# Heads of 64 dimensions alternate over both row halves and two banks, and the decay's steps stand one place later in block 2

## The reference

```python
# block 1, in each of 2 layers: the indexer of the sparse attention
qi = partial_rope(iq.reshape(bsz, seq, 4, 64), positions)         # IDX_HEADS 4, IDX_DIM 64
ki = partial_rope(rms_norm(ik, g_kidx[l]), positions)             # one key of 64 for all heads
rel = relu(einsum('bthd,bsd->bths', qi, ki) * 64 ** -0.5)
score = einsum('bths,bth->bts', rel, w_idx) * 4 ** -0.5           # then top 64 of the keys
# block 2, in each of 2 layers: the decay of the gated delta rule
g = -exp(A_log) * softplus(a + dt_bias)                           # (256 tokens, 4 heads)
gc = cumsum(g in chunks of 64 tokens)
decay = exp(where(incl, gc[t] - gc[j], -inf));  k_end uses exp(gc[-1] - gc)
# and, beside it, silu(causal_conv(q, k, v)) with 4 taps; MoBA attention, 4 heads of 64
```

## Time and profile before

| | |
|---|---|
| median of 3 runs | 1377.88 us (1376.53 to 1378.09) |
| the profiled execution | 1379.59 us, of which the span is 1377.80 us |
| PE busy | 1350.5 us, 98% of the span |
| DVE busy | 1039.6 us, 75% |
| ACT busy | 754.8 us, 55% |
| mean granted clock of PE | 0.996 of full speed |

### The profile page before, as it was taken

The page is one execution under the profiler, slowest core; times in us unless marked ns, Lnnn a source line. Parts: engine busy times, 40 slices in busy tenths (PEclk is TensorE's granted clock), DMA queues, the critical chain, the costliest instruction groups (busy, mean ns, idle before and its releaser), DMA issues. The chain is left out here.

```text
span 1377.8 us, 26466 instructions
## 1 busy us (share of the span) xinstructions
PE 1350.5 (98%) x10812; PEld 1270.2 (92%) x10812; DVE 1039.6 (75%) x1777; ACT 754.8 (55%) x1163; POOL 46.2 (3%) x48
## 2 busy tenths in 40 slices
PE   8999999999999999999999999999999999999998
PEld 8899999998999989899999989999989899888996
DVE  6999898677766667999897767666777746768565
ACT  6544656556445455544567546444558546576463
POOL 0000000000000000000000000000000110001100
PEclk9999999999999999999999999999999999999999
DMA  8555444564655465655355554555463324243231
GB/s 283 184 202 171 135 153 158 180 214 157 203 191 184 144 223 169 210 171 186 100 184 159 196 196 154 185 193 195 162 196 109 120 63 141 94 172 108 78 100 70
DMA packets 108992, 223.77 MB, mean 162 GB/s; under 512 B 6180, under 2 KB 17700, under 8 KB 108872
## 3 DMA queue, kind: packets, MB, share of 16 engines
q1 hardware_dynamic: 106736, 219.12, 48.0%
q10 hardware_dynamic: 2136, 2.96, 0.7%
HBM read 221.01 MB, written 1.06 MB: 161 GB/s over the span
## 5 line engine op out<-in xcount | busy, mean ns | idle before, releaser
L1749 DVE TENSOR_TENSOR wlo<-ring,whi 128x1024 fp32r<-128x1024 f32 (+3 forms) x430 | 498.4, 1181 | 191.6 <-ACT whi L1166 161.9
L1166 ACT ACTIVATE whi<-ring 128x1024 fp32r<-128x1024 f32 (+3 forms) x430 | 433.0, 1026 | 367.1 <-PE bank L497 230.8
L497 PE MATMUL bank<-hhi,whi 128*128 128x256 f32 x2016 | 279.6, 280 | 6.6 <-ACT sgb L1426 4.8
L506 PE MATMUL bank<-hhi,wlo 128*128 128x256 f32 x2016 | 280.3, 281 | 0.0
L497 PE MATMUL bank<-hlo,whi 128*128 128x256 f32 x2016 | 276.9, 279 | 0.0
L497 PEld LDWEIGHTS bank<-hhi,whi 128*128 128x128 f32 x2016 | 253.6, 189 | 10.1 <-ACT sgb L1426 5.5
L506 PEld LDWEIGHTS bank<-hhi,wlo 128*128 128x128 f32 x2016 | 252.6, 188 | 3.7 <-issue 3.2
L497 PEld LDWEIGHTS bank<-hlo,whi 128*128 128x128 f32 x2016 | 253.2, 189 | 0.0
L467 PE MATMUL bank<-w 64*64 64x64 f32 (+5 forms) x1376 | 104.4, 249 | 1.2 <-DMA w<-in_flip 0.8
L1929 DVE SCALAR_TENSOR_TENSOR w<-w,par 128x256 f32<-128x256 f32 x240 | 98.1, 480 | 0.0
L519 PE MATMUL bank<-whi,hhi 128*128 128x512 f32 (+2 forms) x256 | 96.5, 378 | 0.0
(11 more groups left out here) (309 smaller groups left out, 1538.1 us busy)
## 6 DMA issues: line engine op xcount, KB each, us to landing
ring<-in_w_in SPq DMA_DIRECT2D x100, 1024.0 KB, 5.1
ring<-in_w_ffn_down SPq DMA_DIRECT2D x22, 1024.0 KB, 5.1
ring<-in_w_ffn_gate SPq DMA_DIRECT2D x20, 1024.0 KB, 5.1
ring<-in_w_ffn_up SPq DMA_DIRECT2D x20, 1024.0 KB, 5.1
ring<-in_w_merge SPq DMA_DIRECT2D x8, 1024.0 KB, 5.2
ring<-in_w_out SPq DMA_DIRECT2D x8, 1024.0 KB, 4.9
ring<-in_w_oc SPq DMA_DIRECT2D x4, 1024.0 KB, 5.4
ring<-in_w_od SPq DMA_DIRECT2D x4, 1024.0 KB, 5.2
```

What stands on the lines that cost most here:

```text
L497: done = e.matmul(o, wh[:, k, cols(u)], s_[:, k0 + k, :], stop=False, skip_group_check=True, start=opens and k == 0 and s_ is sh and u % 2 ...
L506: done = e.matmul(o, wl[:, k, cols(u)], sh[:, k0 + k, :], start=False, stop=closes, skip_group_check=True)
L1166: e.activation(part_of(whi, j), part_raw(j), ACT.Copy).then_inc(*up("hi.a"))
L1749: e.tensor_tensor(part_of(wlo, j), part_raw(j), part_of(whi, j), ALU.subtract).then_inc(*up("lo.v"))
```

## The change

First, in the indexer of block 1, two query heads are turned at once as one block of 128 columns, and the key is copied twice side by side (a new DVE copy for each of the two token blocks, into `kk`) and turned as a third block. So `iT` holds heads 0 and 2 in its slots 0 and 1 in the lower 64 partitions, heads 1 and 3 in the upper 64, and the key in both. Each token block needs one bank and one evacuation by ACT where it had two. Second, the index scores alternate between the two halves of the partitions and between two banks. Third, `logits_p` takes both banks ahead and, for MoBA, alternates in the same way. Fourth, in block 2 the third and fourth step of the decay stand at places 12 and 13 where they stood at 11 and 12.

```diff
--- before.py
+++ after.py
@@ -93,7 +93,7 @@
         "bias": [5, 5, 5, 6],
         "taps": [12, 20, 34],
         "others": [28, 34, 41, 41, 53],
-        "decay": [10, 10, 11, 12],
+        "decay": [10, 10, 12, 13],
         "delta": [17, 18, 20, 20, 30, 30, 36, 37, 39, 41, 43, 46, 46, 48, 48, 50, 51, 52, 53, 54, 55, 62, 65, 66, 66],
         "latent": [26, 29, 30, 34, 36, 37, 39, 43, 46, 53, 54, 65, 66],
         "outs": [58, 66, 71, 71],
@@ -252,7 +252,9 @@
 
         A1, B1, vAf = part1(0, 1024), part1(1024, 1024), part1(2048, 1024)
         ibuf = blocks(part1(3072, 648))
-        iT = part1(3720, 1280)[0:64].rearrange("p (h s) -> p h s", h=5)
+
+        iT = part1(3720, 768).rearrange("p (h s) -> p h s", h=3)
+        kk = part1(4488, 256).rearrange("p (t a d) -> p t a d", t=2, a=2)
         mk = c4(part1(5000, 512))
         sqT, skT = c4(part1(5512, 1024)), c4(part1(6536, 1024))
         gpad = part1(5512, 1032).rearrange("p (r c s) -> p r c s", r=2, c=2)
@@ -573,13 +575,15 @@
 
             def logits_p(name, l, tb, tag, qT, kT, rowtiles=False):
                 nk = P * (tb + 1)
-                for hp in range(2):
-                    bk = ps.take(e, "s", tag, "lg", l, tb, hp)
-                    for j in range(2):
-                        h = hp + 2 * j if rowtiles else 2 * hp + j
-                        done = group(bk[:, j * nk:(j + 1) * nk], [(qT(h, tb), kT(h, 0, nk))])
-                    done.then_inc(*up(name))
-                    put(name, tag, "lg", l, tb, hp)
+                bks = [ps.take(e, "s", tag, "lg", l, tb, hp) for hp in range(2)]
+                for n in range(4):
+
+                    hp, j = (n % 2, n // 2) if rowtiles else (n // 2, n % 2)
+                    h = hp + 2 * j if rowtiles else 2 * hp + j
+                    done = group(bks[hp][:, j * nk:(j + 1) * nk], [(qT(h, tb), kT(h, 0, nk))])
+                    if j == 1:
+                        done.then_inc(*up(name))
+                        put(name, tag, "lg", l, tb, hp)
 
             def probs_p(name, l, tag, lg):
                 for tb in range(2):
@@ -627,22 +631,24 @@
                 yield 1
                 for tb in range(2):
                     e.wait_ge(*at("irope", l, tb))
-                    for h0, n in ((0, 4), (4, 1)):
-                        bk = ps.take(e, "s", "iT", l, tb, h0)
-                        for h in range(h0, h0 + n):
-                            done = turn(bk[0:64, cols(h - h0)], ibuf[:, tb, h * 64:h * 64 + 64])
-                        done.then_inc(*up("indexer.p"))
-                        put("indexer.p", "iT", l, tb, h0)
+                    bk = ps.take(e, "s", "iT", l, tb)
+                    for q in range(2):
+                        turn(bk[:, cols(q)], ibuf[:, tb, q * P:q * P + P])
+                    done = turn(bk[:, cols(2)], kk[:, tb].rearrange("p a d -> p (a d)"))
+                    done.then_inc(*up("indexer.p"))
+                    put("indexer.p", "iT", l, tb)
                 for tb, step in ((0, 2), (1, 11)):
                     yield step
                     nk = P * (tb + 1)
                     e.wait_ge(*at("iT", "in", l))
-                    for hp in range(2):
-                        bk = ps.take(e, "s", "isc", l, tb, hp)
-                        for j in range(2):
-                            done = group(bk[:, j * nk:(j + 1) * nk], [(iT[:, 2 * hp + j, cols(tb)], iT[:, 4, 0:nk])])
-                        done.then_inc(*up("indexer.p"))
-                        put("indexer.p", "isc", l, tb, hp)
+                    bks = [ps.take(e, "s", "isc", l, tb, hp) for hp in range(2)]
+                    for j in range(2):
+                        for hp in range(2):
+                            r = slice(64 * hp, 64 * hp + 64)
+                            done = group(bks[hp][:, j * nk:(j + 1) * nk], [(iT[r, j, cols(tb)], iT[r, 2, 0:nk])])
+                            if j == 1:
+                                done.then_inc(*up("indexer.p"))
+                                put("indexer.p", "isc", l, tb, hp)
 
             def sparse_p(l):
                 for tb in range(2):
@@ -1270,12 +1276,10 @@
                     put("indexer.a", "isq", l, tb)
                 yield 1
                 for tb in range(2):
-                    for h0, n in ((0, 4), (4, 1)):
-                        bk = bank("iT", l, tb, h0)
-                        e.wait_ge(*at("iT", l, tb, h0))
-                        e.activation(iT[:, h0:h0 + n, cols(tb)], heads(bk[0:64, 0:n * P], n),
-                                     ACT.Copy).then_inc(*up("indexer.a"))
-                        leave("indexer.a", "iT", l, tb, h0)
+                    e.wait_ge(*at("iT", l, tb))
+                    e.activation(iT[:, :, cols(tb)], heads(bank("iT", l, tb)[:, 0:384], 3),
+                                 ACT.Copy).then_inc(*up("indexer.a"))
+                    leave("indexer.a", "iT", l, tb)
                 put("indexer.a", "iT", "in", l)
 
             def sparse_a(l):
@@ -1993,6 +1997,8 @@
                     e.wait_ge(*now(name))
                     rope_v(name, ibuf[:, tb, 0:320].rearrange("p (h d) -> p h d", h=5), 5, 8, cs[:, tb, 16:24],
                            cs[:, tb, 40:48], mk[:, tb, 0:160].rearrange("p (a h d) -> p a h d", a=4, h=5))
+                    e.wait_ge(*now(name))
+                    e.tensor_copy(kk[:, tb], bc(kx, [P, 2, 64])).then_inc(*up(name))
                     put(name, "irope", l, tb)
                 for tb in range(2):
                     nk = P * (tb + 1)
@@ -2001,7 +2007,7 @@
                         bk = bank("isc", l, tb, hp)
                         e.wait_ge(*at("isc", l, tb, hp))
                         for j in range(2):
-                            h = 2 * hp + j
+                            h = hp + 2 * j
                             e.tensor_scalar(rl[:, h, 0:nk], bk[:, j * nk:(j + 1) * nk], 0.0, ibuf[:, tb, 320 + h:321 + h],
                                             ALU.max, ALU.mult).then_inc(*up(name))
                         leave(name, "isc", l, tb, hp)
```

## The result

The changed kernel takes 1380.74 us against 1377.72, ten runs of each, beside each other: a ratio of 1.0025, 95% interval 1.0014 to 1.0035. That is 3.0 us more than 1377.72 by the medians, or 3.4 by the ratio. A repetition with five runs (after_again), on another chip, gives 1.0035 (1.0022 to 1.0049). One run of 7608 us, at the full granted clock, stands outside and is left out. The profiled execution took 1380.15 us, and its span is 1378.4.

A forecast was written before the change was run, and what follows sets the result against it. PE is busy 98% of the span, but its savings count only if its next wait ends earlier. Block 1 -2.2, clock +0.65 and block 2 +5.0 sum to +3.4 us, 1381.2 against 1377.88; range 1376.8 to 1384.0.

The forecast's parts named there:

- Transposes, scores, copies: Block 1, per layer: transposes 0.45 us less, scores 0.5 and 0.9 less; each new DVE copy 0.23, hidden.
- What reaches the end of block 1: Block 1: only transposes and first scores count, 1.1 us per layer, 2.2 in all; the second scores' 0.9 doesn't.
- The clock behind that wait: Block 1, behind the 169 us wait: clock falls in one layer of two, 1.6 us less 0.94 hidden, +0.65.
- MoBA's order: logits_p: alternating MoBA's logits and taking two banks ahead costs or gains nothing, since they already overlap.
- The rival of the strict order: Block 2's logits_p: matmuls run strictly in program order, so alternation saves 2.8 us; +0.6, 1378.5; chance 0.05.
- Block 2, the waits: Block 2: gsum's 1.85 us wait goes; a wait of some 3.4 us for DVE's copy comes at the transposes.
- Block 2, the chain: Block 2: new whi and wlo delay the last exponential, and the squares move 2.5 us per layer; +5.0 in all.
- the fall: Block 2, behind the new wait at the transposes: PE's clock falls again, but the later chain covers it.
- the fast rival: Block 2: gc is copied ahead of the taps, so waits and two clock falls go, 7.6 us; 1368.1; chance 0.08.

The follow-up runs named there:

- index_only: Changed kernel with the decay's steps back at 10, 10, 11, 12; 0.9984 of the kernel before, and 0.9987 when run once more (index_only_again).
- decay_only: Kernel before with only the decay's steps moved, to 10, 10, 12, 13; 1.0036 of the kernel before, 5.0 us more.
- scores_twice: Changed kernel with the second token block's scores computed twice in each layer of block 1; 1.0032 of the kernel before.
- awake_gct16: Changed kernel with 16 extra matmuls on PE in the wait ahead of block 2's eight transposes; 1.0047 of the kernel before.
- logits_old: Changed kernel with logits_p as before, one bank at a time and MoBA's heads in order 0, 2, 1, 3; 1.0033 of the kernel before.
- decay_first: Changed kernel with the decay ahead of the taps in the table, so DVE copies gsum before the taps; 1.0044 of the kernel before.
- step3_late: Changed kernel with the decay's steps at 10, 10, 11, 13, only the last step moved; 1.0020 of the kernel before, 2.8 us more.
- index_awake8: Changed kernel with the decay's old places and 8 extra matmuls on PE ahead of gsum; 0.9985 of the kernel before.

## Why the prediction was right

Forecast +3.4 us and 1381.2; measured +3.0 to +3.4 and 1380.74. Its two large terms were each measured alone: -2.2 for block 1 (index_only -2.2 and -1.8), +5.0 for block 2 (decay_only +5.0). The mechanism held: a longer chain over ACT and DVE in block 2, and a part of block 1's saving lost in a wait. Two smaller terms were off in opposite directions, and that the total hits to a few tenths is luck.

**Transposes, scores, copies.** 0.45 was 0.43; 0.5 and 0.9 were 0.5 and 0.9. MoBA's rows were the right price for the index scores. A new copy on DVE takes 0.23 us, as estimated.

**What reaches the end of block 1.** The sum, 1.1 us per layer, came out, the reason only half. In layer 0 PE begins the part behind the second scores at 125.53 us, before at 127.42: 1.89 ahead, 0.24 of which it had from the first part (12.32 against 12.56), so 1.65 is saved. At 169 us it is 1.39 ahead: 1.15 come through, and 0.49 are in the longer wait. The step that failed here: the prediction let nothing of the second scores pass and the wait grow by 0.6. scores_twice shows that some 0.4 of 0.86 pass. DVE was idle for 0.59 of these 34 us, which leaves room for it, but which of DVE's steps follows PE's scores was not traced.

**The clock behind that wait.** Forecast: a fall in one layer of two, 0.65 net. The odds were right: of the 22 layers in the eleven profiles of kernels with a wait of some 1.97 us there, 10 had a fall behind it; of 6 with the old wait of 1.48, none. The price was not. By the time of the part that begins 12 us behind the wait, a fall has delayed PE by the 1.5 to 1.6 us that were forecast. But the next wait for `sgb` stands 26.8 us behind the first and hides more than its 0.94 us: with the restart the gap there is 1.0 to 1.2 us, and where the projection runs at the faster of its two paces (last section) PE loses 0.4 us more in short gaps ahead of it, which are gone behind a fall (10.5 and 10.1 us for the same parts, without a fall and with one). So in eight of the ten layers with a fall nothing was left of it at that point. The changed kernel with a fall in layer 0 and index_only without, from 167.61 and 167.63 us on:

```profile
194.42 1.16 PE L499 MATMUL bank<-hhi,whi 128*128 128x256 f32 x8
```

```profile
194.43 1.18 PE L499 MATMUL bank<-hhi,whi 128*128 128x256 f32 x8 [0.87 <-ACT sgb L1430]
```

In the two others (layer 0 of index_only_again and of awake_gct16), at the slower pace, 0.5 us arrived. In the changed kernel the +0.65 is 0.

**MoBA's order.** Nothing, as forecast: logits_old. The rival of the strict order falls with it: heads written 0, 2, 1, 3 take the time of 0, 1, 2, 3.

**Block 2, the waits.** The wait of `gsum` is gone in layer 0 and 0.7 us in layer 1; the new one is 3.80 us, forecast 3.4. In block 1 the wait at 169 us is 1.97 us, forecast 2.1.

**Block 2, the chain.** Forecast 2.5 us per layer; measured up to the squares 2.8 and 3.1 in the first profile and 3.1 and 2.4 in the second, and 2.8, 3.1, 3.0 and 2.4 up to the later wait. The last exponential starts 10.35 us behind `wlo`, forecast 10.4. The forecast's chain alone ends 15.8 us behind `wlo` (58.8 - 43.0); awake_gct16, which takes the clock out, has 15.65. The term that was mis-sized is the fall: the prediction had one of 3.4 us, wholly covered. Where it is 3.4 us long, in layer 0 of decay_only and layer 1 of after_again, it is covered, and PE waits 0.5 and 0.7 us at the squares (in decay_only the clock then fell once more behind that wait, and the layer cost 3.9 us). In the eight other layers with this order it is 6.6 us or longer, and 0.1 to 0.9 us of it show; in the changed kernel, 0.4 and 0.7. Without the 0.65 of block 1 and with 2.8 and 3.1 in the two layers the sum is 5.9 - 2.2 = +3.7; small errors of opposite sign stand in the forecast's +3.4.

**Why the fast rival failed.** It took the wait and the low clock for the whole cost. decay_first gives it most of its condition, the copy ahead of the taps, though not a transposition without a wait (1.39 us are left), and is not faster: the chain is still 14.30 us, PE's next wait comes at the squares, and in layer 0 the clock falls there.

Of the versions without extra matmuls index_only is the best: the change without its fourth part, 1.8 to 2.2 us faster than the kernel before.

## What to carry to other kernels

Time taken from the busiest engine counts only up to its next wait for a chain that did not move; read that wait before and after, for it shows a few tenths that the time can't. When a step moves by one place, list what each engine's queue now runs ahead of it: here six taps (1.35 us) and one pair of `whi` and `wlo` (1.7 us) made the chain 3.1 us longer per layer, while the removed wait with its low clock had cost 0.7. And read an interval past the next waits too: a kernel that is only 1.0 us late at its next step (step3_late) can lose another 1.6 behind it, when PE waits there and its clock falls. Filling a wait to keep the clock up helps only if the engine isn't early for the next one.

## What the runs showed of the hardware that had not been expected

The fall of TensorE's clock has no fixed length. Behind the same wait of 1.9 us ahead of `gsum` it was at half for 3.4 us in index_only_again and for 6.6 in index_only; behind 2.85 us in decay_first for 9.8 us. Nor does the length of the wait decide whether it falls: behind the waits of 1.48 to 1.50 us at 169 us and in layer 1 it fell in none of six layers, but behind the 1.02 us at the squares in both layers of step3_late, and behind 0.39 us in layer 1 of index_awake8, where the 0.38 us of layer 0 had no fall. What decides was not found.

At full clock the projection's matmuls have two paces. The same stage, block 1's second feed-forward net, in two executions of the changed kernel, start, us, instructions:

```profile
838.70 1.07 PE L508 MATMUL bank<-hhi,wlo 128*128 128x256 f32 x8
839.60 1.07 PE L499 MATMUL bank<-hhi,whi 128*128 128x256 f32 x8
```

```profile
842.36 1.11 PE L508 MATMUL bank<-hhi,wlo 128*128 128x256 f32 x8
843.30 1.10 PE L499 MATMUL bank<-hhi,whi 128*128 128x256 f32 x8
```

Eight matmuls of 128x256 take 0.90 us in the one and 0.94 in the other, 113 and 118 ns each, with the granted clock at 1.00. The pace changes within an execution too: in this same stage after_again goes over to the faster one by 890 us, while the changed kernel's first profile keeps the faster and the trace of before the slower one throughout. From the stage's first part (830.01 us before, 828.63 after) to the first matmul of line 519 (521) at 998.48 and 992.46 us the changed kernel gained 4.6 us, with nothing changed there. This is why single profiles of one kernel differ by several us, why the span after (1378.4) is only 0.6 longer than before, and why the stages were compared by intervals within them. What sets the pace was not found.
